# The same two transformer blocks with the order of the on-chip tiles changed

## The chip, the cores and the metric

One core of a Trainium2 chip runs the whole program. The metric is the time of one execution on the device in microseconds (us); the figure for a kernel is the median of its runs.

## The reference

Two transformer blocks, each of width 1024, work in float32 on a sequence of 512 tokens. Cut to what matters:

```
# block 1
hn   = rmsnorm(h) * g_mix;  rq, rk, rv, rg, fq, fk, fv, ff = split(hn @ w_in)
ret  = silu(rg) * group_norm(chunk_retention(rotary(rq), rotary(rk), rv))     # 8 heads of 64
fox  = forgetting_attention(rmsnorm(fq), rmsnorm(fk), fv, log_sigmoid(ff+b))  # 8 heads of 64, causal
h   += concat(ret, fox) @ w_out
h   += memory_cross_attention(rmsnorm(h), mem, ...) @ w_xo                    # 4 heads of 256, 256 memory rows
h   += (silu(hn @ w_gate) * (hn @ w_up)) @ w_down                             # 2816 wide
# block 2
9 modulation vectors = silu(c) @ w_ada + b_ada                                # 1024 x 9216 weights
x   += 0.5 * gt1 * swiglu(modulate(rms_norm(x)), w1_gu, w1_down)              # 2816 wide
proj = modulate(rms_norm(x)) @ w_in      # short convolution branch, sliding window attention branch (16 heads)
x   += gt2 * (merged @ w_out)
x   += 0.5 * gt3 * swiglu(modulate(rms_norm(x)), w2_gu, w2_down)
return rms_norm(x)
```

## The kernel before

**Tiling.** Activations stand feature by token: 128 partitions by 512 tokens is a chunk of 2 KiB a partition, and 1024 features are 8 chunks. All dense weights are cut beforehand into 343 units of 128 by 1024 floats (8 weight tiles of 128 by 128, 4 KiB a partition). `units` in memory holds them in the order of use.

**Each product is done in three passes.** A float32 weight unit `raw` is split into a high part `whi` (rounded to fp32r by ScalarE, L389) and a low part `wlo = raw - whi` (GpSimd, L363). Activations are split likewise: `xh`/`xl`, `yh`/`yl`, `hh`/`hl`, `oh`/`ol`. TensorE then adds whi·xh, whi·xl and wlo·xh in a PSUM bank, so a unit is 24 matmuls. In most layers the two passes with `whi` come first (L1298, L1299) and the pass with `wlo` last (L1304). In the three down projections the three passes alternate (L1398 to L1400) and a unit waits for its `wlo` before its first matmul. 16 of the 343 units (memory keys and values) have 256 columns, all others 512.

**Rings and queues.** SyncE (SP) loads unit u into one of four slots of `raw` once the low part of unit u - 4 has been made. `whi` and `wlo` have two slots each: ScalarE splits unit u once TensorE has used unit u - 2, and GpSimd follows it. VectorE evacuates the banks, makes the low halves of the activations (L906, L931: `hl <- tmp, hh`), adds the residual into `h` (L880, L882) and the sums of squares into `ssum` (L798). ScalarE makes the high halves (L515, L454), the squares (L437) and the functions. Between the parts stands a norm: the squares of eight chunks, column sums on TensorE (L1426, L1427), a root on ScalarE (L444), a reciprocal on VectorE (L807), a spread over the partitions on TensorE (L1436), and then chunk by chunk `xn` (L823), `xh` (L454) and `xl` (L817), which the first two units of the next layer follow (L1275 to L1277). During the layer `gu` VectorE also works through `w_ada` (L956), which SP loads into `ada_w`.

**Tiles on the chip.** Every tile is a range of bytes of all 128 partitions, and `sb(...)` (L123) gives them out one after the other, each at a multiple of 32 bytes; the first begins at byte 2,176. `arena` is 88 KiB that the stages use in turn: `proj`, `memh`/`meml`, `mem_in`, `kmem`, `vmem`, `xq`, `hh` (44 KiB from its start), `hl` (the 44 KiB after it), `yh` (0), `yl` (16), `conv`/`m1` (32), `qkv` (48), `oh` (56), `kdup` (72) and others are placed in it by `at(...)` at a fixed distance from `arena_at`. `side` is 12 KiB, used in the same way from `side_at` (`ada_w`, `lt`, `rb`, `rh`, `cpad`, `pt_sw`). Two further fixed starts are used: `x_at` (the start of `xh`; `pt_a` and `pt_b` are laid over `xh`/`xl`) and `xn_at` (`ol_b` is laid over `xn`, `ssum` and `rstd`).

```
arena_kb = 88
arena = sb("arena", arena_kb * 256)
arena_at = nc.sbuf_base - arena_kb * 1024
...
def at(name, kb, cols, dt=f32, base=arena_at):
    return nc.alloc_sbuf_tensor_at(name, [P, cols], dt, offset=base + int(kb * 1024))
```

Of the kernel before, what the change touches and what calls it, by code (L numbers as in the profile page):

```python
# [21 lines left out]
T = 512  # L22
M = 256
P = 128
C = D // P
# [13 lines left out]
UNIT = 8 * P  # L39
# [77 lines left out]
def two_block_kernel(nc, x_t, mem_t, units, w_ada, vectors, tables, decays, out_t):  # L117
    f32, f32r = mybir.dt.float32, mybir.dt.float32r
# [3 lines left out]
    with ExitStack() as ctx:  # L122
        def sb(name, cols, dt=f32):  # L123
            return ctx.enter_context(nc.sbuf_tensor(name, [P, cols], dt))
# [2 lines left out]
            return ctx.enter_context(nc.semaphore(name))  # L127


        arena_kb = 88  # L130
        arena = sb("arena", arena_kb * 256)
        arena_at = nc.sbuf_base - arena_kb * 1024
        x_at = nc.sbuf_base
        xh, xl = sb("xh", C * T, f32r), sb("xl", C * T, f32r)
        whi, wlo = sb("whi", 2 * UNIT, f32r), sb("wlo", 2 * UNIT, f32r)
        raw = sb("raw", 4 * UNIT)
        h = sb("h", C * T)
        tmp = sb("tmp", 4 * T)
        xn_at = nc.sbuf_base
        xn = sb("xn", 2 * T)  # L140
# [7 lines left out]
        mods = sb("mods", NMOD * C)  # L148
        gmod = sb("gmod", 6 * C + 1 + C)
        dec = sb("dec", 4 * T)  # L150
        side = sb("side", 12 * 256)
        side_at = nc.sbuf_base - 12 * 1024

        def at(name, kb, cols, dt=f32, base=arena_at):
            return nc.alloc_sbuf_tensor_at(name, [P, cols], dt, offset=base + int(kb * 1024))
# [1820 lines left out]
def build(nc, arrays):  # L1976
    aps = {k: nc.dram_tensor(k, list(v.shape), mybir.dt.float32, kind="ExternalInput").ap() for k, v in arrays.items()}
    out_t = nc.dram_tensor("out_t", [D, T], mybir.dt.float32, kind="ExternalOutput").ap()
    two_block_kernel(nc, *[aps[k] for k in ("x_t", "mem_t", "units", "w_ada", "vectors", "tables", "decays")], out_t)
# [11 lines left out]
```

## Time and profile before

| | |
|---|---|
| median of 3 runs | 2235.74 us (2231.91 to 2236.38) |
| profiled execution, its own time | 2235.74 us |
| its span, first to last instruction | 2233.9 us |
| mean granted clock of TensorE | 0.981 of full speed |
| TensorE busy with matmuls | 2138.2 us, 96% of the span |
| VectorE, ScalarE, GpSimd busy | 883.8, 704.8, 836.8 us |
| moved by DMA | 228.09 MB, mean 102 GB/s |

A busy share is an average over stages. Matmuls overlap in the records (their ends are modelled), so the distance between starts tells the pace, not the length of a record. In the rows below PE is TensorE's matmuls, PEld its weight loads, DVE VectorE, ACT ScalarE, POOL GpSimd. A q behind a name is that engine's queue.

### The profile page before, as it was taken

Reading aid. Unit: us, or ns where it says so; the run is one execution under the profiler, and the core shown is the slowest. Engines: PE = TensorE matmul, PEld = TensorE weight load, DVE = VectorE, ACT = ScalarE, POOL = GpSimd, SP = SyncE. Lnnn points to the kernel's source line nnn. Section 1 sums busy time; section 2 is a strip of 40 time slices with the busy share of each in tenths; the row PEclk is TensorE's granted clock in tenths of the full one; section 3 lists DMA queues with packets and bytes.
Section 4 is the critical chain, followed back from the end, with each engine's and each line's share of the span. In section 5 each row is a group of like instructions: output and inputs, shape, how many; then the busy total and the mean of one; then the engine's idle time right before and its main releaser. Section 6 shows DMA issues by size and latency. Waiting matters only on the chain.

```text
span 2233.9 us, 27520 instructions
## 1 busy us (share of the span) xinstructions
PE 2138.2 (96%) x10024; PEld 1735.7 (78%) x10024; DVE 883.8 (40%) x1143; ACT 704.8 (32%) x1063; POOL 836.8 (37%) x347
## 2 busy tenths in 40 slices
PE   8998889989899999999999989999999999999998
PEld 6777678868778778788888878877777887888886
DVE  3555765243767763132221131453333324222111
ACT  4233344233222222232232232223454223322221
POOL 3333223404344444334444434433222443444443
PEclk9999999999999999999999999999999998999999
DMA  5232212203566754222322223322111332332231
GB/s 186 79 111 78 76 48 67 88 17 104 188 217 205 229 194 141 85 85 94 99 98 94 94 67 104 106 82 85 45 50 44 98 95 75 101 96 94 96 102 67
DMA packets 68855, 228.09 MB, mean 102 GB/s; under 512 B 7600, under 2 KB 8880, under 8 KB 68784
## 3 DMA queue, kind: packets, MB, share of 16 engines
q1 hardware_dynamic: 66848, 223.83, 30.9%
q10 hardware_dynamic: 1936, 3.25, 0.5%
q8 instruction: 51, 0.84, 0.2%
q14 instruction: 20, 0.16, 0.0%
HBM read 223.91 MB, written 2.10 MB: 101 GB/s over the span
## 4 chain that ended last, share of the span: by engine, by line
issue 67%; POOL 27%; PE 5%; POOLq 1%; DVE 0%; ACT 0%; DVEq 0%
POOL wlo L363 27%; PE bank L1398 2%; PE bank L1400 2%; PE bank L1399 2%; POOLq L362 0%; POOLq L366 0%; DVE h L1258 0%; DVE ssum L798 0%; POOLq L363 0%; PE bank L1436 0%; PE bank L1426 0%; PE bank L1427 0%; DVE h L882 0%; DVEq L122 0%; ACT tmp L437 0%
## 5 line engine op out<-in xcount | busy, mean ns | idle before, releaser
L363 POOL TENSOR_TENSOR wlo<-raw,whi 128x1024 fp32r<-128x1024 f32 x343 | 836.6, 2439 | 1376.1 <-ACT whi L389 1376.0
L1298 PE MATMUL bank<-xh,whi 128*128 128x512 f32 x1664 | 656.7, 395 | 5.2 <-ACT whi L389 5.2
L1299 PE MATMUL bank<-xl,whi 128*128 128x512 f32 x1664 | 650.7, 391 | 0.0
L389 ACT ACTIVATE whi<-raw 128x1024 fp32r<-128x1024 f32 x343 | 362.3, 1056 | 717.9 <-PE bank L1304 409.5
L1304 PE MATMUL bank<-xh,wlo 128*128 128x512 f32 x1664 | 411.2, 389 | 0.0
L1298 PEld LDWEIGHTS bank<-xh,whi 128*128 128x128 f32 x1664 | 314.4, 189 | 73.3 <-issue 5.6
L1299 PEld LDWEIGHTS bank<-xl,whi 128*128 128x128 f32 x1664 | 314.2, 189 | 65.7 <-issue 1.4
L1304 PEld LDWEIGHTS bank<-xh,wlo 128*128 128x128 f32 x1664 | 312.3, 188 | 65.2
L1398 PE MATMUL bank<-hh,whi 128*128 (+1 forms) x528 | 206.0, 390 | 1.7 <-POOL wlo L363 1.6
L1400 PE MATMUL bank<-hh,wlo 128*128 (+1 forms) x528 | 205.5, 389 | 0.0
L1399 PE MATMUL bank<-hl,whi 128*128 (+1 forms) x528 | 205.4, 389 | 0.0
L926 DVE TENSOR_TENSOR tmp<-tmp,bank 128x512 f32<-128x512 f32 x52 | 35.8, 688 | 353.8 <-ACT tmp L524 353.8
L1398 PEld LDWEIGHTS bank<-hh,whi 128*128 128x128 f32 x528 | 99.1, 188 | 23.5 <-POOL wlo L363 3.0
L956 DVE SCALAR_TENSOR_TENSOR xn<-ada_w,gmod,xn 128x768 f32<-128x768 f32 x84 | 115.1, 1371 | 5.2 <-DMA ada_w<-w_ada 1.9
L524 ACT ACTIVATE tmp<-bank 128x512 f32<-128x512 f32 x60 | 35.9, 599 | 253.4 <-PE bank L1304 251.8
L1400 PEld LDWEIGHTS bank<-hh,wlo 128*128 128x128 f32 x528 | 99.1, 188 | 20.6
L1399 PEld LDWEIGHTS bank<-hl,whi 128*128 128x128 f32 x528 | 99.1, 188 | 20.4
L931 DVE TENSOR_TENSOR hl<-tmp,hh 128x512 f32 (+1 forms) x44 | 95.9, 2179 | 40.2 <-ACT hh L515 40.2
L882 DVE SCALAR_TENSOR_TENSOR h<-bank,gmod,h 128x512 f32<-128x512 f32 x16 | 12.0, 747 | 207.4 <-PE bank L1400 200.1
L1298 PE MATMUL bank<-yh,whi 128*128 128x512 f32 x216 | 86.9, 402 | 0.0
L1299 PE MATMUL bank<-yl,whi 128*128 128x512 f32 x216 | 85.1, 394 | 0.0
L1275 PE MATMUL bank<-xh,whi 128*128 128x512 f32 x104 | 46.4, 447 | 19.8 <-DVE xl L801 10.8
(252 smaller groups left out, 2201.1 us busy)
## 6 DMA issues: line engine op xcount, KB each, us to landing
raw<-units SPq DMA_DIRECT2D x343, 512.0 KB, 3.5
ada_w<-w_ada SPq DMA_DIRECT2D x96, 384.0 KB, 4.0
h<-x_t SPq DMA_DIRECT2D x8, 256.0 KB, 6.0
dec<-decays ACTq DMA_DIRECT2D x8, 256.0 KB, 3.3
out_t<-h SPq DMA_DIRECT2D x8, 256.0 KB, 2.1
mem_in<-mem_t SPq DMA_DIRECT2D x1, 1024.0 KB, 12.0
kdup<-qkv ACTq DMA_DIRECT2D x8, 128.0 KB, 2.8
tab<-tables SPq DMA_DIRECT2D x1, 832.0 KB, 8.2
```

What stands on the lines that cost most here:

```text
L363: pool.tensor_tensor(wlo[:, j % 2 * UNIT:(j % 2 + 1) * UNIT], raw[:, j * UNIT:(j + 1) * UNIT], whi[:, j % 2 * UNIT:(j % 2 + 1) * UNIT].bit ...
L389: act.activation(whi[:, v % 2 * UNIT:(v % 2 + 1) * UNIT], raw[:, slot * UNIT:(slot + 1) * UNIT], ACT.Copy).then_inc(hi_ready, 1)
L524: act.activation(chunk(tmp, s), banks[j - 1 + member][:, :], func).then_inc(acted, 1)
L931: tt(chunk(split_to[1], g), t, chunk(split_to[0], g).bitcast(f32), ALU.subtract).then_inc(half_lo, 1)
L956: stt(acc[:, 0:ADA_W], w, csilu[:, k:k + 1], acc[:, 0:ADA_W], ALU.mult, ALU.add).then_inc(ada_step, 1)
L1275: mm(bank[:, 0:n], wh, rh_, start=t == 0, stop=False)
L1298: mm(bank[:, 0:n], wh, chunk(rhs[0], t, n), start=t == 0, stop=False)
L1299: mm(bank[:, 0:n], wh, chunk(rhs[1], t, n), start=False, stop=False)
L1304: last = mm(bank[:, 0:n], wlo[:, slot * UNIT + t * P:slot * UNIT + (t + 1) * P], chunk(rhs[0], t, n), start=False, stop=t == 7)
L1398: mm(bank[:, :], wh, rh_, start=first and kk == 0, stop=False)
L1399: mm(bank[:, :], wh, rl_, start=False, stop=False)
L1400: done = mm(bank[:, :], wl, rh_, start=False, stop=last_unit and kk == 1)
```

## The change

No instruction is added, removed or put elsewhere in a queue. The list of `sb(...)` calls is put in another order: `h` comes first, then `xh`, `xl`, then `raw`, `whi`, `wlo`, then the small tiles from `tmp` to `dec` in their old order, and `side` and `arena` stand last. `arena_at` and `side_at` are worked out from the end.

```
-        arena_kb = 88
-        arena = sb("arena", arena_kb * 256)
-        arena_at = nc.sbuf_base - arena_kb * 1024
+        h = sb("h", C * T)
         x_at = nc.sbuf_base
         xh, xl = sb("xh", C * T, f32r), sb("xl", C * T, f32r)
-        whi, wlo = sb("whi", 2 * UNIT, f32r), sb("wlo", 2 * UNIT, f32r)
-        raw = sb("raw", 4 * UNIT)
-        h = sb("h", C * T)
+        raw, whi, wlo = sb("raw", 4 * UNIT), sb("whi", 2 * UNIT, f32r), sb("wlo", 2 * UNIT, f32r)
         tmp = sb("tmp", 4 * T)
...
         dec = sb("dec", 4 * T)
+        arena_kb = 88
         side = sb("side", 12 * 256)
-        side_at = nc.sbuf_base - 12 * 1024
+        arena = sb("arena", arena_kb * 256)
+
+        end = nc.sbuf_base
+        arena_at = end - arena_kb * 1024
+        side_at = arena_at - 12 * 1024
```

From the sizes, the first byte of each tile in a partition:

| tile | KiB | starts before | starts after | moved by |
|---|---|---|---|---|
| arena | 88 | 2,176 | 132,096 | +126.875 KiB |
| h | 16 | 157,824 | 2,176 | -152 KiB |
| xh, xl | 16 each | 92,288 | 18,560 | -72 KiB |
| raw | 16 | 141,440 | 51,328 | -88 KiB |
| whi, wlo | 8 each | 125,056 | 67,712 | -56 KiB |
| tmp, xn, ssum, rstd and the small tiles to dec | 36.7 | 174,208 | 84,096 | -88 KiB |
| side | 12 | 209,920 | 119,808 | -88 KiB |

The last byte in use is the same, 222,208.

## Rows read from the trace of the kernel before

**Rows 1.** The page: span, busy time and instructions of each engine.
```profile
span 2233.9 us, 27520 instructions
PE 2138.2 (96%) x10024; PEld 1735.7 (78%) x10024; DVE 883.8 (40%) x1143; ACT 704.8 (32%) x1063; POOL 836.8 (37%) x347
```

**Rows 2.** The waits of PE: reader, releaser, total us, times, longest.
```profile
PE bank L1275 <- DVE xl L801: 10.8, 2, 8.8
PE bank L1796 <- DVE xn L956: 10.4, 10, 3.8
PE bank L1426 <- ACT tmp L437: 8.7, 4, 2.7
PE bank L1275 <- DVE xl L817: 7.4, 3, 2.5
```

**Rows 3.** One line's or tile's instructions: duration in ns, min/median/max, first and last start.
```profile
L1298 PE MATMUL bank<-xh,whi x135: 389/389/389, 1089.7 to 1179.4; 128*128 128x512 f32 x135
L1398 PE MATMUL bank<-hh,whi x163: 389/389/393, 1199.8 to 1310.0; 128*128 x96, 128*128 128x512 f32 x67
L1298 PE MATMUL bank<-yh,whi x54: 389/389/389, 1809.8 to 1844.7; 128*128 128x512 f32 x54
L1298 PE MATMUL bank<-oh,whi x56: 389/389/389, 1727.8 to 1796.2; 128*128 128x512 f32 x56
```

**Rows 4.** Timeline: start us, us, engine, line, what, idle before; once per unit or pair of units.
```profile
1008.60 0.69 DVE L926 TENSOR_TENSOR tmp<-tmp,bank 128x512 f32<-128x512 f32 x1 [7.11 <-ACT tmp L524]
...
1149.96 0.69 DVE L926 TENSOR_TENSOR tmp<-tmp,bank 128x512 f32<-128x512 f32 x1 [6.95 <-ACT tmp L524]
...
1210.73 2.40 POOL L363 TENSOR_TENSOR wlo<-raw,whi 128x1024 fp32r<-128x1024 f32 x1 [3.04 <-ACT whi L389]
...
1297.77 2.40 POOL L363 TENSOR_TENSOR wlo<-raw,whi 128x1024 fp32r<-128x1024 f32 x1 [3.04 <-ACT whi L389]
...
1815.01 0.75 DVE L882 SCALAR_TENSOR_TENSOR h<-bank,mods,h 128x512 f32<-128x512 f32 x1 [4.69 <-PE bank L1304]
...
1842.21 0.75 DVE L882 SCALAR_TENSOR_TENSOR h<-bank,mods,h 128x512 f32<-128x512 f32 x1 [4.09 <-PE bank L1304]
```

**Rows 5.** The same view as rows 3, of ACT, DVE and POOL over the span.
```profile
L389 ACT ACTIVATE whi<-raw x343: 1038/1060/1077, 4.6 to 2209.7; 128x1024 fp32r<-128x1024 f32 x172
L515 ACT ACTIVATE hh<-tmp x66: 619/633/636, 561.8 to 2101.8; 128x512 f32 x60, 128x512 fp32r<-128x512 f32 x6
L454 ACT ACTIVATE xh<-xn,mods x24: 722/723/726, 948.6 to 1865.5; 128x512 fp32r<-128x512 f32 x24
L817 DVE SCALAR_TENSOR_TENSOR xl<-xn,mods,xh x24: 745/747/753, 949.4 to 1866.3; 128x512 fp32r<-128x512 f32 x24
L880 DVE TENSOR_TENSOR h<-bank,h x24: 678/692/693, 359.4 to 940.3; 128x512 f32<-128x512 f32 x24
L363 POOL TENSOR_TENSOR wlo<-raw,whi x343: 2340/2397/3116, 5.8 to 2210.8; 128x1024 fp32r<-128x1024 f32 x172
L931 DVE TENSOR_TENSOR hl<-tmp,hh x44: 691/2240/2472, 967.3 to 2102.6; 128x512 f32 x40, 128x512 fp32r<-128x512 f32 x4
```

**Rows 6.** Timeline of POOL and DVE in layer gu1, and of DVE in az.
```profile
998.55 2.39 POOL L363 TENSOR_TENSOR wlo<-raw,whi 128x1024 fp32r<-128x1024 f32 x1 [3.54 <-ACT whi L389]
999.27 2.22 DVE L931 TENSOR_TENSOR hl<-tmp,hh 128x512 f32 x1 [0.95 <-ACT hh L515]
...
1009.50 2.40 POOL L363 TENSOR_TENSOR wlo<-raw,whi 128x1024 fp32r<-128x1024 f32 x1 [3.61 <-ACT whi L389]
1010.21 2.24 DVE L931 TENSOR_TENSOR hl<-tmp,hh 128x512 f32 x1 [0.92 <-ACT hh L515]
...
1755.28 0.69 DVE L931 TENSOR_TENSOR yl<-tmp,yh 128x512 f32 x1 [0.90 <-ACT yh L515]
```

**Rows 7.** DMA issues: KB each, median us from issue to landing.
```profile
raw<-units SPq DMA_DIRECT2D x343, 512.0 KB, 3.5
ada_w<-w_ada SPq DMA_DIRECT2D x96, 384.0 KB, 4.0
```

**Rows 8.** Instructions of L515 in layer gu, and then in layer gu1.
```profile
L515 ACT ACTIVATE hh<-tmp x20: 630/633/634, 561.8 to 793.2; 128x512 f32 x19, 128x512 fp32r<-128x512 f32 x1
...
L515 ACT ACTIVATE hh<-tmp x19: 621/634/636, 966.6 to 1161.7; 128x512 f32 x18, 128x512 fp32r<-128x512 f32 x1
```

**Rows 9.** Stretches: PE busy (records), PEclk, DMA share, GB/s.
```profile
700.00:750.00 50.00, 48.53 (x225) 1.00 0.64 210
1000.00:1050.00 50.00, 50.00 (x223) 1.00 0.28 94
1850.00:1900.00 50.00, 46.90 (x194) 0.86 0.23 69
```

## The prediction

> **What bounds the kernel now.** I read the busy times first [rows 1]: TensorE has matmuls in flight for 2138.2 of 2233.9 us, so only 2233.9 - 2138.2 = 95.7 us of the span are not covered by it. The waits of PE [rows 2] say where much of that lies: the starts of layers behind a norm (L1275 waiting for `xl`, L1426 for the squares) and the small sums of the modulation vectors (L1796). Everything else is the pace of the matmuls. That pace I take from the distance between starts of something that comes once per unit or pair of units [rows 4]. In gu1, L926 comes every second unit: from 1008.60 to 1149.96 are 13 steps, 26 units, so 141.36 / 26 = 5.437 us a unit. In down1, L363 comes every unit: 16 steps from 1210.73 to 1297.77, 87.04 / 16 = 5.440 us. In out2, L882: 5 steps from 1815.01 to 1842.21, 27.20 / 5 = 5.440 us. A unit has 24 matmuls, so each takes 226.7 ns. 327 of the 343 units have 512 columns: 327 x 5.44 = 1779 us, four fifths of the span, go at this one pace. The granted clock in such a stretch is 1.00; it is 0.86 where a norm has just interrupted TensorE [rows 9].
>
> So there are two ways in which a change of place can reach the time: the pace of the matmuls, to which the kernel is very sensitive, and the 95.7 us in which VectorE, ScalarE and TensorE wait for each other.
>
> **The change part by part.** It removes and adds no instruction, wait or transfer. What changes is the address field of nearly every one of them, so each term of the sum is (number of instructions) x (change of the duration of one with its address), and the question to the trace is whether any duration there depends on the address. The kernel before has its tiles all over the partition, which makes it a fair test of itself.
>
> *TensorE.* Its moving operands lie at very different places and distances from `whi` (125,056): `yh` is at 2,176, `hh` from 2,176 to 47,232, `hl` from there to 92,288, `oh` at 59,520, `xh` at 92,288. The matmuls on each have the same recorded duration, median 389 ns in all four stretches [rows 3], and the pace, which is the better measure, is 5.437, 5.440 and 5.440 us a unit with `xh`, `hh` and `yh` [rows 4]. Those three differ by 0.003 us at most, and 0.003 x 327 = 1.0 us. After the change `xh` lies 48 KiB below `whi` where it lay 32 KiB below, and `hh` 63 KiB above where it lay 120 KiB below; these pairs are new, but of the same kind as those which show nothing. Term: 0, bounded by 1 us either way as far as the stages can tell. The far bound, for pairs that were never seen: the longest record in down1 is 393 ns against 389 [rows 3]. If all 327 x 24 = 7,848 matmuls took 4 ns more, that would be +31 us; as much less would be -31 us. I take 0, because the rows nearest to the case are the three paces.
>
> *ScalarE.* The split L389 is 1038 to 1077 ns over 343 instructions that go round all slots of `raw` and `whi`; L515 writes 22 chunks of `hh` over 44 KiB and has 619 to 636 ns; L454 writes `xh` in 722 to 726 ns [rows 5]. The spread is at most 3% and the layers repeat it. Each of these lies beside the matmuls in the dense layers, and on the path in the norms. Term: 0.
>
> *VectorE.* L817 has 745 to 753 ns, L880 678 to 693 [rows 5]. If all the uncovered time were made of such work and all of it moved from the median to an end, it would change by (747 - 745) / 747 to (753 - 747) / 747, that is -0.3% to +0.8% by L817, and by -2% (678 against 692) by L880. On 95.7 us this is -1.9 to +0.8 us. Term: 0, bounds -2 and +1 us.
>
> *VectorE against GpSimd.* One duration does vary: L931 takes 0.69 us when alone and 2.2 us when a split L363 is running [rows 5, 6]. The two readings are an exclusion in time and a collision in place. The rows favour the first: begun 0.72 us after L363, L931 ends at 1001.49 and L363 at 1000.94; the next time it ends at 1012.45 and L363 at 1011.90. Both times it ends 0.55 us behind the end of L363, with `hh` and `hl` a chunk further on. Term: 0. If it were a collision in place and the change removed it, 44 + 22 instructions (L931 in gu1 and gu2, L906 in gu) would each be 1.5 us shorter, 100 us of VectorE's time, and the total would still not move: VectorE is idle for 7 us before the next L926 [rows 4], and that is the cover. What it costs where the cover is gone is one such wait per norm, 1.5 us.
>
> The Trainium skill, page "SBUF — State Buffer", section "Who interferes with whom", has the rule: VectorE with two SBUF inputs and GpSimd reading SBUF exclude each other for the whole instruction, and by it nothing else among the engines contends. By that rule the trace agrees (the end 0.55 us behind) and the term is 0; by the other reading it would be the 100 us of VectorE's time just worked out, and still 0 on the path.
>
> *GpSimd.* L363 is 2340/2397/3116 ns [rows 5], and idles 3.04 us before each in down1 [rows 4]. The chain of one unit there is L389 (1.06) and L363 (2.40) inside a unit of 5.44, so it has 5.44 - 1.06 - 2.40 = 1.98 us to spare. Even the longest L363 (+0.72) does not use it up. Term: 0.
>
> *Transfers.* A unit lands 3.5 us after its issue [rows 7] and the ring is four units, 21.8 us, deep. All tiles outside `arena` move by whole KiB, so how their bytes lie to any power of two up to 1 KiB is unchanged, `raw` and `ada_w` included; `arena` moves from 128 above a multiple of 256 to a multiple of 1024. Only `mem_in`, the window table and `kdup` are transferred there, all far ahead of their readers. That transfers do not disturb engines is seen in L515: 633 ns in gu, beside 210 GB/s, and 634 ns in gu1 [rows 8], beside 94 GB/s; the stretches at 700 and 1000 us stand for the two layers [rows 9]. Term: 0.
>
> *Sum.* 0 + 0 + 0 + 0 + 0 + 0 against the profiled 2235.74 us (span 2233.9 and 1.84 around it), which is also the median of the three runs. Prediction: 2235.7 us, with -3 to +2 us from the bounds of what stages show (1 us for TensorE, -2 to +1 for the rest). The three runs of before spread over 4.47 us, 0.2% of the time, so 0.2% is about what a measurement can tell from no change.
>
> **The rivals.**
>
> *Slower: operands that collide.* Place: a weight load from `whi` or the split's traffic (`raw`, now just below `whi`) beside a moving operand at a distance that the kernel before never had. Price: 7,848 x the delay of one. It decides from 4.5 / 7,848 = 0.57 ns a matmul, a quarter of a per cent of 226.7 ns; at the 4 ns of the widest record it gives 2235.7 + 31 = 2267 us. For it: the sensitivity, and that the new distances are untested. Against it: four operands at four distances with the same 389 ns, and three equal paces.
>
> *Faster: a collision that is there already and goes.* The same place and the same 0.57 ns with the other sign; at -4 ns, 2204 us. Against it: a collision would have to weigh equally on `xh`, `yh`, `hh` and `oh` to leave the paces equal, and then on what the four have in common, the traffic among `raw`, `whi` and `wlo`, whose order also changes (the pair `whi`, `wlo` keeps its distance, `raw` goes from above them to below). I find this a little less likely than the slower one.
>
> *The uncovered time shifts.* The terms in the norms all fall at one end: -2 us, 2234 us, which reads as no change.
>
> *Longer programs.* Addresses formed in registers in the loops might need one more instruction now that `arena` starts beyond 128 KiB. Rows of this case don't price it; the count of instructions would leave 27520.
>
> **How the numbers follow.** No change 0.79, of which the shifted uncovered time is a part; slower by collisions (or longer programs) 0.12; faster 0.09. The bound of the stages, 2233 to 2238, widened by the scatter of the runs (-3.8 and +0.6 us around the median, taken as 4 either way) is 2229 to 2242; it holds the case without change nearly whole and the weakest form of both rivals.
>
> **What would show it right or wrong.** Right: 27520 instructions, 5.44 us from L926 to L926 halved in gu1 and from L363 to L363 in down1, L931 still near 2.24 us, L454 at 723 and L817 at 747 ns, PE idle near 96 us. Wrong: a pace other than 5.44 in one layer but not in others (then the operand names the colliding pair), or a changed duration of L389 or L363 (then the split's tiles), or a sum of PE waits behind norms that moved by more than 4 us.

## The result, and the profile after

The changed kernel takes 2247.73 us (median of 4 runs, 2247.17 to 2248.75). The kernel before takes 2233.82 us (4 runs, 2230.99 to 2236.38; the three runs given before the prediction are among them). The ratio is 1.0063 with a 95% interval of 1.005 to 1.0076: slower by 13.9 us, outside the range of the prediction. Against the medians of the kernel before in the later comparisons (2235.33, 2234.80 and 2234.80 us, 13 to 15 runs each) the same 2247.73 us is 12.4 to 12.9 us more. The profiled execution has 2246.83 us and a span of 2245.0 us, 11.1 us more than the span of [rows 1].

The page of the kernel after:

```profile
span 2245.0 us, 27520 instructions
PE 2151.8 (96%) x10024; PEld 1734.8 (77%) x10024; DVE 883.2 (39%) x1143; ACT 704.7 (31%) x1063; POOL 836.2 (37%) x347
```

As many instructions as before. VectorE, ScalarE and GpSimd are busy as long as before to 0.7 us; TensorE's matmuls are in flight 13.6 us longer (2151.8 against 2138.2). So the time lies in matmuls, not in waits: the uncovered part went from 95.7 to 2245.0 - 2151.8 = 93.2 us.

Where, the paces tell. Timeline of the kernel after, at the places of [rows 4] (all line numbers are one higher): L927 in gu1, where `xh` and `xl` are read; L364 in down1 (`hh`, `hl`); L883 in out2 (`yh`, `yl`):

```profile
1011.11 0.69 DVE L927 TENSOR_TENSOR tmp<-tmp,bank 128x512 f32<-128x512 f32 x1 [7.11 <-ACT tmp L525]
...
1130.71 0.69 DVE L927 TENSOR_TENSOR tmp<-tmp,bank 128x512 f32<-128x512 f32 x1 [6.95 <-ACT tmp L525]
...
1219.13 2.40 POOL L364 TENSOR_TENSOR wlo<-raw,whi 128x1024 fp32r<-128x1024 f32 x1 [3.20 <-ACT whi L390]
...
1303.13 2.40 POOL L364 TENSOR_TENSOR wlo<-raw,whi 128x1024 fp32r<-128x1024 f32 x1 [3.20 <-ACT whi L390]
...
1833.83 0.75 DVE L883 SCALAR_TENSOR_TENSOR h<-bank,mods,h 128x512 f32<-128x512 f32 x1 [4.18 <-PE bank L1305]
...
1856.24 0.75 DVE L883 SCALAR_TENSOR_TENSOR h<-bank,mods,h 128x512 f32<-128x512 f32 x1 [4.25 <-PE bank L1305]
```

gu1 has 11 steps of two units in 119.60 us, 5.436 us a unit, the old pace. (Its steps alternate between 10.80 and 10.96 us in both kernels, so an odd number of them, here and in the prediction, comes out a little low; two steps together are 21.76 us in both, 5.440 us a unit.) down1 has 15 units in 84.00 us, 5.600 us. out2 has 4 units in 22.41 us, 5.603 us. A unit that reads the arena takes 0.16 us more, 6.7 ns on each of its 24 matmuls (233.3 against 226.7 ns); a unit that reads `xh` takes none. The idle time of GpSimd before each split in down1 has grown by the same 0.16 us, from 3.04 to 3.20. It waits for ScalarE's split, which waits until TensorE has used unit u - 2.

Recorded durations of matmuls in the kernel after (min/median/max in ns), one operand each, to be held against [rows 3], where the median is 389 everywhere:

```profile
L1299 PE MATMUL bank<-xh,whi x131: 389/389/389, 1094.9 to 1184.6; 128*128 128x512 f32 x131
L1399 PE MATMUL bank<-hh,whi x164: 392/394/500, 1195.1 to 1309.4; 128*128 x96, 128*128 128x512 f32 x68
L1299 PE MATMUL bank<-yh,whi x56: 398/398/398, 1816.8 to 1853.7; 128*128 128x512 f32 x56
L1299 PE MATMUL bank<-oh,whi x56: 391/396/398, 1734.1 to 1803.5; 128*128 128x512 f32 x56
```

`hh`, `yh` and `oh` lie in the arena, `xh` does not. The others are as in [rows 5] and [rows 6]:

```profile
L390 ACT ACTIVATE whi<-raw x343: 1039/1059/1079, 4.6 to 2219.7; 128x1024 fp32r<-128x1024 f32 x172
L364 POOL TENSOR_TENSOR wlo<-raw,whi x343: 2339/2396/3053, 5.8 to 2220.8; 128x1024 fp32r<-128x1024 f32 x172
L455 ACT ACTIVATE xh<-xn,mods x24: 721/722/727, 951.1 to 1873.4; 128x512 fp32r<-128x512 f32 x24
L818 DVE SCALAR_TENSOR_TENSOR xl<-xn,mods,xh x24: 743/747/752, 951.8 to 1874.2; 128x512 fp32r<-128x512 f32 x24
L932 DVE TENSOR_TENSOR hl<-tmp,hh x44: 691/2240/2474, 969.8 to 2109.6; 128x512 f32 x40, 128x512 fp32r<-128x512 f32 x4
...
1012.02 2.40 POOL L364 TENSOR_TENSOR wlo<-raw,whi 128x1024 fp32r<-128x1024 f32 x1 [3.61 <-ACT whi L390]
1012.72 2.24 DVE L932 TENSOR_TENSOR hl<-tmp,hh 128x512 f32 x1 [0.92 <-ACT hh L516]
```

The sum. Units that read the arena and run at TensorE's pace: xq 8, xo 8, the three down layers 66, az 8 (of 16), out2 8, together 98, and 98 x 0.16 = 15.7 us. By the marks of the norms (the first root of each, L444 before and L445 after) the segment with gu1 and down1 grew from 372.43 to 375.67 us, +3.2 of 22 x 0.16 = 3.5; the five segments from xq on grew by 1.6, 1.5, 3.2, 2.2 and 2.5 us, 11.0 together. So the count gives the size of the loss only roughly: 15.7 us, where the medians give 12.4 to 13.9 and the two profiled executions 11.0. Two segments account for most of the gap: the one with xq and xo (1.6 of 2.6 us) and the one with gu and down (1.5 of 3.5). Part of it is the price itself: in the first down layer ten splits take 54.40 us before (875.21 to 929.61) and 55.76 after (877.49 to 933.25), 0.136 us a unit and not 0.16. The remainder was not followed up. Eight units of cz also read the arena (`yh`, `yl`), beside the attention, and are left out of the count.

### The profile page after: what moved, and what is told of

It is laid out like the page before. It is cut to its first block, busy times and chain, and to the rows that moved or that the text cites. A ratio compares the mean times of both kernels' runs of the same rounds, so it can differ in the third digit from the quotient of the medians.

```text
span 2245.0 us, 27520 instructions
## 1 busy us (share of the span) xinstructions
PE 2151.8 (96%) x10024; PEld 1734.8 (77%) x10024; DVE 883.2 (39%) x1143; ACT 704.7 (31%) x1063; POOL 836.2 (37%) x347
## 4 chain that ended last, share of the span: by engine, by line
PE 61%; issue 27%; POOL 10%; DVE 1%; ACT 0%; POOLq 0%; DVEq 0%; ACTq 0%
PE bank L1299 13%; PE bank L1300 12%; PE bank L1305 12%; POOL wlo L364 10%; PE bank L1399 5%; PE bank L1401 5%; PE bank L1400 5%; PE bank L1842 2%; PE bank L1855 1%; PE bank L1276 1%; PE bank L1278 1%; PE bank L1277 1%; PE bank L1843 1%; PE bank L1848 1%; PE bank L1437 0%
## 5 line engine op out<-in xcount | busy, mean ns | idle before, releaser
L364 POOL TENSOR_TENSOR wlo<-raw,whi 128x1024 fp32r<-128x1024 f32 x343 | 836.0, 2437 | 1386.8 <-ACT whi L390 1386.7
L927 DVE TENSOR_TENSOR tmp<-tmp,bank 128x512 f32<-128x512 f32 x52 | 35.8, 688 | 354.0 <-ACT tmp L525 354.0
L932 DVE TENSOR_TENSOR hl<-tmp,hh 128x512 f32 (+1 forms) x44 | 95.9, 2179 | 40.1 <-ACT hh L516 40.1
L883 DVE SCALAR_TENSOR_TENSOR h<-bank,gmod,h 128x512 f32<-128x512 f32 x16 | 12.0, 748 | 213.6 <-PE bank L1401 206.0
```

Source lines behind the costliest of these rows:

```text
L364: pool.tensor_tensor(wlo[:, j % 2 * UNIT:(j % 2 + 1) * UNIT], raw[:, j * UNIT:(j + 1) * UNIT], whi[:, j % 2 * UNIT:(j % 2 + 1) * UNIT].bit ...
L932: tt(chunk(split_to[1], g), t, chunk(split_to[0], g).bitcast(f32), ALU.subtract).then_inc(half_lo, 1)
```

## The experiments

All compare with the kernel before on the same chip. `sb("pad...", n)` puts 4n unused bytes between tiles.

Below, the residue of a tile is what is left of its first byte after division, to 256 if nothing else is said: 2,176 is 8 x 256 + 128, so its residue is 128.

**The first four: which property of the arena's new place.** The arena has moved above 128 KiB, it has moved from 128 above a multiple of 1024 to a multiple of 1024, and `raw`, `whi` and `wlo` have changed order and distance.

e1, the new residue at the old height:

```
+        sb("pad0", 224)
         arena = sb("arena", arena_kb * 256)
         arena_at = nc.sbuf_base - arena_kb * 1024
+        sb("pad1", 32)
```

> The kernel before, with 896 bytes of padding ahead of the arena and 128 behind it: the arena starts at 3,072, a multiple of 1024, as after the change, but stays at the low end; everything else moves up by exactly 1 KiB. Theory ALIGNMENT (a moving operand that starts at a multiple of 256, not 128 above one like the weights, costs 6.7 ns a matmul): down1 goes at 5.60 us a unit instead of 5.44, total 2246 to 2248 us. Theory HIGH ADDRESS (a moving operand above 128 KiB of the partition costs it): down1 stays at 5.44 us and the total at 2231 to 2236 us. Theory NEIGHBOURS (the new order or distance of raw, whi and wlo costs it): also 5.44 us, 2231 to 2236 us.

e2, the changed kernel with the old residue:

```
         side = sb("side", 12 * 256)
+        side_at = nc.sbuf_base - 12 * 1024
+        sb("pad0", 32)
         arena = sb("arena", arena_kb * 256)
-
-        end = nc.sbuf_base
-        arena_at = end - arena_kb * 1024
-        side_at = arena_at - 12 * 1024
+        arena_at = nc.sbuf_base - arena_kb * 1024
```

> The changed kernel, with 128 bytes of padding ahead of the arena: it starts at 132,224, which is 128 above a multiple of 1024 like before the change, and stays at the high end. ALIGNMENT: down1 returns to 5.44 us a unit, total 2231 to 2236 us. HIGH ADDRESS: 5.60 us, 2246 to 2248 us. NEIGHBOURS: 5.60 us, 2246 to 2248 us.

e3, the arena in the middle, across 128 KiB:

```
+        h = sb("h", C * T)
+        x_at = nc.sbuf_base
+        xh, xl = sb("xh", C * T, f32r), sb("xl", C * T, f32r)
         arena_kb = 88
         arena = sb("arena", arena_kb * 256)
         arena_at = nc.sbuf_base - arena_kb * 1024
-        x_at = nc.sbuf_base
-        xh, xl = sb("xh", C * T, f32r), sb("xl", C * T, f32r)
-        whi, wlo = sb("whi", 2 * UNIT, f32r), sb("wlo", 2 * UNIT, f32r)
-        raw = sb("raw", 4 * UNIT)
-        h = sb("h", C * T)
+        raw, whi, wlo = sb("raw", 4 * UNIT), sb("whi", 2 * UNIT, f32r), sb("wlo", 2 * UNIT, f32r)
```

> Order h, xh, xl, arena, raw, whi, wlo and the rest: the arena from 51,328 to 141,440, residue 128 kept, so that only hl chunks 17 to 21 lie above 131,072; raw, whi and wlo in the changed order but at the old heights (141,440 to 174,208). HIGH ADDRESS with its edge at 128 KiB: the units of a down layer stay at 5.44 us except the last two or three of each half (about 5.49 us, as only one pass in three reads hl), total within 2 us of the kernel before. With an edge lower down more units would be slow, and the first slow unit tells where it is. ALIGNMENT: 5.44 us throughout, as before. NEIGHBOURS by order (raw below whi): 5.60 us, about 2247 us.

e4, `xh` and `xl` at the top:

```
-        x_at = nc.sbuf_base
-        xh, xl = sb("xh", C * T, f32r), sb("xl", C * T, f32r)
         whi, wlo = sb("whi", 2 * UNIT, f32r), sb("wlo", 2 * UNIT, f32r)
...
         side_at = nc.sbuf_base - 12 * 1024
+        sb("pad0", 32)
+        x_at = nc.sbuf_base
+        xh, xl = sb("xh", C * T, f32r), sb("xl", C * T, f32r)
```

> The kernel before with xh and xl as the last tiles (189,568 and 205,952, residue 128) and the arena still lowest. HIGH ADDRESS: the 221 units that read xh and xl go at 5.60 us, those that read the arena at 5.44 us, total about 2234 + 221 x 0.16 = 2269 us. ALIGNMENT and NEIGHBOURS: 5.44 us everywhere, 2231 to 2236 us.

Measured: e1 2247.43 us, ratio 1.0052 (1.0035 to 1.0069). e2 2234.94 us, ratio 1.000 (0.999 to 1.001). e3 2234.37 and e4 2234.55 us, one execution each, against 2235.33 us for the kernel before (the figures in brackets are 95% intervals). The timeline of L365 in down1 of e1, and of L363 in e2:

```profile
1215.75 2.40 POOL L365 TENSOR_TENSOR wlo<-raw,whi 128x1024 fp32r<-128x1024 f32 x1 [3.20 <-ACT whi L391]
...
1299.74 2.40 POOL L365 TENSOR_TENSOR wlo<-raw,whi 128x1024 fp32r<-128x1024 f32 x1 [3.20 <-ACT whi L391]
```

```profile
1215.71 2.40 POOL L363 TENSOR_TENSOR wlo<-raw,whi 128x1024 fp32r<-128x1024 f32 x1 [3.04 <-ACT whi L389]
...
1297.31 2.40 POOL L363 TENSOR_TENSOR wlo<-raw,whi 128x1024 fp32r<-128x1024 f32 x1 [3.04 <-ACT whi L389]
```

15 units each: 83.99 us (5.599 a unit) with the arena low but at a multiple of 1024, 81.60 us (5.440) with it high but 128 above. The height, the order and the distance do nothing that these times show (e2, e3 and e4 lie 0.4 to 1.0 us under the kernel before); 128 bytes of padding give back the whole loss. HIGH ADDRESS and NEIGHBOURS fall. ALIGNMENT stands, but in two forms: the place of the moving operand by itself, or against that of the weights, which are 128 above a multiple of 256 in all four kernels and in the changed one.

**The next four: absolute or relative, and how fine.** f1 moves the arena, `xh`, `xl`, `whi`, `wlo` and `raw` to multiples of 1024 together; f2 moves only `whi` and `wlo` there; f3 and f4 give the arena, `xh` and `xl` other residues and keep the weights at 128.

```
# f1: one pad ahead of all of them
+        sb("pad0", 224)
         arena = sb("arena", arena_kb * 256)
...
         raw = sb("raw", 4 * UNIT)
+        sb("pad5", 32)
# f2
+        sb("pad3", 224)
         whi, wlo = sb("whi", 2 * UNIT, f32r), sb("wlo", 2 * UNIT, f32r)
+        sb("pad4", 32)
# f3 (f4: pad0 232, pad3 8)
+        sb("pad0", 8)
         arena = sb("arena", arena_kb * 256)
...
+        sb("pad1", 8)
         x_at = nc.sbuf_base
-        xh, xl = sb("xh", C * T, f32r), sb("xl", C * T, f32r)
+        xh = sb("xh", C * T, f32r)
+        sb("pad2", 8)
+        xl = sb("xl", C * T, f32r)
+        sb("pad3", 232)
```

> The kernel before with the arena, xh, xl, whi, wlo and raw all at multiples of 1024 (they stood 128 above one). Theory ABSOLUTE (a matmul takes 6.7 ns more whenever its moving operand starts at a multiple of 256): now the 221 units that read xh and xl are slow too: all units 5.60 us, total about 2247 + 221 x 0.16 = 2283 us, a little less where it is hidden. Theory RELATIVE (the cost comes from moving operand and weights having different residues): 5.44 us everywhere, 2231 to 2236 us.

> The kernel before with only whi and wlo at multiples of 1024, all moving operands still 128 above one. ABSOLUTE: 5.44 us everywhere, 2231 to 2236 us. RELATIVE: 5.60 us everywhere, about 2283 us.

> The kernel before with the arena 160, xh 192 and xl 224 bytes above a multiple of 1024, weights at 128. Read by the starts of single matmuls: whi*xh, whi*xl in a dense layer and the down layers. ABSOLUTE: all as before (226.7 ns a matmul, 5.44 us a unit) unless the step needs 128 exactly. RELATIVE: all slow, 233.3 ns. If the cost grows with the distance to an edge (for instance as the number of lines of some size that 2048 bytes touch), the three residues differ.

> The same with the arena 32, xh 64 and xl 96 above a multiple of 1024. ABSOLUTE with exact multiples only: all 5.44 us. If it is the half of a 256-byte line in which the operand starts (0 to 127 slow, 128 to 255 fast): all 5.60 us, total about 2283 us. RELATIVE: all 5.60 us.

Measured: f1 2233.76 us, ratio 0.9998 (0.9988 to 1.0007). f2 2272.13, f3 2270.64, f4 2273.87 us, one execution each against 2234.8, at granted clocks of 0.981 to 0.982, as before. With all at multiples of 1024 nothing is lost, and moving the weights alone makes every unit slow though no moving operand was touched. Timeline of f2, first L928 in gu1, which reads `xh`, then L365 in down1:

```profile
1007.99 0.69 DVE L928 TENSOR_TENSOR tmp<-tmp,bank 128x512 f32<-128x512 f32 x1 [7.22 <-ACT tmp L526]
...
1130.77 0.69 DVE L928 TENSOR_TENSOR tmp<-tmp,bank 128x512 f32<-128x512 f32 x1 [7.38 <-ACT tmp L526]
...
1220.68 2.40 POOL L365 TENSOR_TENSOR wlo<-raw,whi 128x1024 fp32r<-128x1024 f32 x1 [3.44 <-ACT whi L391]
...
1304.34 2.40 POOL L365 TENSOR_TENSOR wlo<-raw,whi 128x1024 fp32r<-128x1024 f32 x1 [3.19 <-ACT whi L391]
```

That is 122.78 us for 22 units, 5.581 us each, where the kernel after has 119.60, and 83.66 us for 15 units, 5.577 us. In f3 down1, with the arena only 32 bytes away from the weights' residue, takes 5.600 us a unit; in f4 it takes 5.62. The expected 2283 us for all units slow was 9 to 12 us too much. In f2 a unit costs 0.137 us more and not 0.16, which is 327 x 0.023 = 7.5 of its 11 us; the rest, and all of it in f4, was not followed up (that it lies in layers where TensorE also waits is likely, not shown). The seven residues tried against the weights' are 32, 64, 96, 128, 160, 192 and 224 bytes, and each layer with any of them is slow. ABSOLUTE falls; the cost belongs to the difference.

f1 holds a further test of this that was not planned. In the layer az the low part of the operand has two homes: `ol_a` in the arena and `ol_b` laid over `xn`. f1 moves the arena and the weights to multiples of 1024 and leaves `xn` 128 above, so `ol_b` alone disagrees with the weights. The timeline of TensorE in f1:

```profile
1749.39 0.39 PE L1300 MATMUL bank<-oh,whi 128*128 128x512 f32 x1
1749.62 0.40 PE L1301 MATMUL bank<-ol_b,whi 128*128 128x512 f32 x1
1749.85 0.39 PE L1300 MATMUL bank<-oh,whi 128*128 128x512 f32 x1
```

By the starts in ns that the trace keeps, the 21 intervals from `ol_b` to the next `oh` are 234 to 235 ns in f1, where they are 226 to 227 in the kernel before and in g3, which puts `xn` at a multiple of 256 too. The 31 intervals from `oh` to `ol_b` are 225 to 227 ns in f1. ScalarE and GpSimd write `whi` and `wlo` in the same stretch, and the `oh` intervals between those of `ol_b` stay short, so the cost follows the operand of the single matmul and not the traffic of the other engines.

**The last three: which modulus, which matmul, and whether more is to be had.** g1 puts the arena, `xh` and `xl` 256, 512 and 768 bytes away from the weights' residue to 1024 (four pads of 64 floats in the places of f3). g2 moves `wlo` alone. g3 is f1 with `h`, `tmp`, `xn`, `ssum`, `rstd` and the constant tables at multiples of 256 too.

```
# g2
-        whi, wlo = sb("whi", 2 * UNIT, f32r), sb("wlo", 2 * UNIT, f32r)
+        whi = sb("whi", 2 * UNIT, f32r)
+        sb("pad0", 224)
+        wlo = sb("wlo", 2 * UNIT, f32r)
+        sb("pad1", 32)
# g3, beside f1 without its pad5
+        sb("pad6", 56)
         tab = sb("tab", NTAB - 2 * P)
...
+        sb("pad7", 40)
         dec = sb("dec", 4 * T)
```

> The kernel before with the arena 384, xh 640 and xl 896 bytes above a multiple of 1024, weights at 128: the differences to the weights are 256, 512 and 768. If the residue that counts is that to 256 bytes, all units go at 5.44 us and the total is 2231 to 2236 us. If it is that to 512 bytes, xh is fine and arena and xl are not: down1 5.60 us, gu1 about 10.88 + 1/3 of 0.32 = 10.99 us a pair, total about 2260 us. If only one place to 1024 were free of cost, all would be slow (about 2271 us); the 512-byte steps of the weight tiles inside a unit speak against that.

> The kernel before with only wlo moved to a multiple of 1024; whi and all moving operands stay 128 above one. One matmul of three then has a weight tile whose residue differs from that of the moving operands: about 5.44 + 0.16/3 = 5.49 us a unit, total about 2234 + 13 = 2247 us, if the cost belongs to single matmuls. In the down layers the order is whi.hh, whi.hl, wlo.hh. OWN PAIR: the interval from the start of wlo.hh to the next start is the long one (233 ns, others 227). OVERLAP (the load of the next weights beside the streaming of the present operand): the interval from whi.hl to wlo.hh is the long one, because wlo is loaded while hl streams.

> All tiles to which TensorE goes for 512-column work at multiples of 256: the f1 layout, with h, tmp, xn, ssum, rstd and the constant tables (tab, 160 above a multiple of 256 in all kernels so far) also at multiples of 256. If the few hundred matmuls that use tab (rotations, head sums, transposes, norm spreads) pay too, at most some 400 x 7 ns = 2.8 us are gained against the kernel before, most of it hidden: 2230 to 2234 us, ratio 0.998 to 1.000. If not, ratio 1.000.

g1: 2235.61 us, and 81.60 us for 15 units in down1, 5.440: the residue to 256 bytes is what counts. Timeline of L368 in g1:

```profile
1216.12 2.40 POOL L368 TENSOR_TENSOR wlo<-raw,whi 128x1024 fp32r<-128x1024 f32 x1 [3.04 <-ACT whi L394]
...
1297.72 2.40 POOL L368 TENSOR_TENSOR wlo<-raw,whi 128x1024 fp32r<-128x1024 f32 x1 [3.04 <-ACT whi L394]
```

g2: 2255.09 us, 20 us more than before where 13 were expected. Timeline of g2: L366 in down1, and three of the matmuls there:

```profile
1221.07 2.40 POOL L366 TENSOR_TENSOR wlo<-raw,whi 128x1024 fp32r<-128x1024 f32 x1 [3.15 <-ACT whi L392]
...
1304.27 2.40 POOL L366 TENSOR_TENSOR wlo<-raw,whi 128x1024 fp32r<-128x1024 f32 x1 [3.15 <-ACT whi L392]
...
1230.07 0.39 PE L1401 MATMUL bank<-hh,whi 128*128 x1
1230.30 0.40 PE L1402 MATMUL bank<-hl,whi 128*128 x1
1230.53 0.40 PE L1403 MATMUL bank<-hh,wlo 128*128 x1
```

The weights of the next matmul are loaded beside the present one: the load for wlo.hh begins at 1230.30, with whi.hl.

```profile
1230.30 0.19 PEld L1403 LDWEIGHTS bank<-hh,wlo 128*128 128x128 f32 x1
```

83.20 us for 15 units is 5.547 us, 0.107 more than 5.440: not 8 but 16 of the 24 matmuls pay, 6.7 ns each on average. The starts in the timeline have steps of 0.01 us; the trace keeps them in ns, and over the 129 or 130 intervals of each kind from 1210 to 1300 us the means are 226.7 ns from whi.hh to whi.hl, 232.4 ns from whi.hl to wlo.hh, and 234.2 ns from wlo.hh to whi.hh. The interval behind whi.hl is long although both its own operands agree; the tile then loaded is of `wlo`. The interval behind wlo.hh is long although the tile then loaded, of `whi`, agrees with `hh`; its own weights do not. The simplest rule that fits g2, f1 and f2 is that a matmul pays when its moving operand disagrees with its own weights or with the next ones, and that in f2, where it disagrees with both, it pays once. OWN PAIR and OVERLAP each explained one of the two. The rule holds for sums over neighbours better than for single matmuls: in az of the kernel after, where `oh` and `ol_a` disagree with the weights and `ol_b` agrees, the interval from `oh` to `ol_a` is 236.3 ns and the one from `ol_a` to `oh` 227.8, where the rule has 233.3 for both, and the one from `ol_b` to `oh` is 229.9 where it has 226.7. The two pairs sum to 464.1 and 461.7 ns, where it has 466.6 and 460.0. Why the parts shift is open. By the count of the rule a dense unit in g2 has 9 slow matmuls (8 with `wlo` and the one before), 9 x 6.7 = 60 ns: L929 of gu1 stands at 1005.88 and, 28 units on, at 1159.69, 5.493 us a unit, 53 ns over 5.440.

g3: 2234.58 us (11 runs, 2230.42 to 2235.35), ratio 0.9998 (0.9989 to 1.0007). The matmuls that use the tables give nothing back. No version beats the kernel before; f1 and e2 beat the changed one by the whole difference.

## Why the prediction was wrong

- **The failed step** is the term of TensorE, "0, bounded by 1 us either way as far as the stages can tell", with the sentence above it that the kernel before is "a fair test of itself". It tested heights and distances, which do nothing (e2, e3, e4). It could not test the residue: all the operands named there, and the weights, were 128 above a multiple of 256. Four equal medians and three equal paces came from operands that were equal in the one property that counts. (The 0.003 us between the paces, from which the bound of 1 us was made, came from the odd number of alternating steps in gu1, not from an operand.) In place of 0, give or take 1 us, the runs show 0.16 us a unit in down1 and out2, and 13.9 us in all.
- The change of that property was seen and put in the wrong paragraph. Under *Transfers* stands that the arena moves "from 128 above a multiple of 256 to a multiple of 1024"; it was asked only which transfers go there, and not which engine reads there, against tiles whose residue stays.
- The rival "Slower: operands that collide" named the right engine, the right pair (a weight load beside a moving operand) and the sensitivity. Its price was 4 ns on 7,848 matmuls; measured are up to 6.7 ns on 98 x 24 = 2,352 of them, 15.7 us by count, 13.9 us by the medians. What it said of distances never had before was not the cause. Its chance, 0.12, was too low for a price that decides from 0.57 ns.
- ScalarE, VectorE and GpSimd at 0 were right: medians within 1 ns of [rows 5]. So was the reading of the 2.2 us of L931 as exclusion in time: in the kernel after, L932 ends at 1014.96 and L364 at 1014.42, again 0.54 us behind, with all its tiles elsewhere.
- The uncovered time stayed, 93.2 us against the 96 foreseen. The programs did not get longer: 27520 instructions.
- The sign that was to show it wrong did: "a pace other than 5.44 in one layer but not in others (then the operand names the colliding pair)". gu1 stayed, down1 and out2 did not.

What stays open is what makes 256 bytes the unit, and why the price varies (below). The runs show the rule for these fp32r matmuls of 512 columns, at a grain of 32 bytes; finer residues, other types and lengths other than 512 and the 256 below were not tried.

## What to carry to other kernels

For matmuls like these, keep the tiles from which TensorE takes weights and moving operands at one residue to 256 bytes; fewer than 256 unused bytes do it, and small tiles of odd sizes allocated ahead of a big buffer undo it without a sign in the program. When a trace is used as its own test for whether a property matters, first check that the property varies in it. And where one engine sets the pace of thousands of equal instructions, take its pace per layer from starts of something that comes once a unit: 3% of a matmul was plain there, and hidden in busy shares of 96% both times.

## What the runs showed of the hardware

- A matmul of 512 columns in fp32r follows the last after 226.7 ns when its moving operand starts at the same residue to 256 bytes as the weights in use and those loaded next. When it does not, the mean over 120 to 200 such intervals lies between 231 and 234 ns. Where one operand is read through one pass, the means by the distance of its residue from that of the weights are: 32 bytes 233.3 ns (down1 in f3), 64 bytes 230.9 (`xh` with `wlo` in gu1, f3), 128 bytes 232.4 (down1 in f2) and 233.3 (down1 after), 160 bytes 234.3 (down1 in f4), 192 bytes 232.4 (`xh` with `wlo` in gu1, f4). So the price is 4 to 8 ns, and not a function of the distance alone.
- The height in the partition (first bytes from 2,176 to 205,952) and the distance made no difference (e2, e3, e4: 2234.37 to 2234.94 us).
- The recorded weight loads are 188 ns in the median either way; only the starts and the matmul records (median 389 ns before against 394 to 398 on the arena's operands after) show it.
- On matmuls of 256 columns the cost is not to be seen: from memh.whi to meml.whi the median of 122 intervals is 120 ns before, after and in e1.
- The Trainium skill, page "SBUF — State Buffer", section "Who interferes with whom", gives TensorE two independent read ports, one for the moving operand and one for weight loads, and says that it never waits on anyone. Against other engines no run here contradicts it. Between its own two reads f2 speaks against "independent": moving the weights by 896 bytes, and with them no other tile's residue, cost 37 us (one execution). Here the measurement decides.
